# A chunked recurrence scan on one core: where one tile's products and one tile's turning stand among the steps of a matrix inverse

## The reference, cut to what matters

```python
def step(S, inp):
    d_t, k_t, v_t, kk_t, a_t = inp[:5]
    sa = jnp.einsum("bhvk,bhk->bhv", S, -kk_t)
    S = (S * d_t[:, :, None, :] + sa[..., None] * (kk_t * a_t)[:, :, None, :]
         + v_t[..., None] * k_t[:, :, None, :])
    out = jnp.einsum("bhvk,bhk->bhv", S, inp[5]) if emit else None
    return S, out
```

## Time and profile before

| what | value |
|---|---|
| runs of the kernel before | 2920.4 us median of 3 (2919.72 to 2921.86) |
| the profiled execution's own time | 2917.95 us |
| its span, first to last instruction | 2916.1 us |
| mean granted TensorE clock | 0.941 |
| PE busy / PEld busy | 89% / 68% of the span |
| DVE / ACT / POOL busy | 53% / 39% / 26% |
| the scan | about 1118 to 1818 us from the span's start |
| the profiled chain of work that ended last | names only the last instructions, so it says nothing of the scan |

### The profile page before, as it was taken

One profiled execution on the slowest core, in us unless ns is written; L12 is line 12 of the kernel. 1 busy time (PEld: TensorE's weight loads), 2 busy tenths in 40 slices (PEclk: granted clock), 3 DMA queues, 4 the chain that ended last, 5 costly groups with the idle time before them and its releaser, 6 DMA issues. The chain is left out here.

```text
span 2916.1 us, 66292 instructions
## 1 busy us (share of the span) xinstructions
PE 2599.0 (89%) x28644; PEld 1989.8 (68%) x28644; DVE 1542.1 (53%) x2689; ACT 1140.8 (39%) x1795; POOL 748.9 (26%) x436
## 2 busy tenths in 40 slices
PE   7998899979899996888888887989999999898987
PEld 5776588747678784777776775757788655476745
DVE  4634578883752313566565653334540366515995
ACT  4633332242452433455454443334422344423333
POOL 2413200002112125555444540122223200041201
PEclk9999899989789897899999998989999999999998
DMA  4224334233444441111111100542312100144431
GB/s 154 86 71 134 136 112 121 76 117 115 165 146 152 163 141 64 42 42 53 37 52 52 31 15 30 202 152 66 115 58 80 58 1 1 56 132 143 136 89 58
DMA packets 83661, 266.38 MB, mean 91 GB/s; under 512 B 11824, under 2 KB 12848, under 8 KB 82992
## 3 DMA queue, kind: packets, MB, share of 16 engines
q1 hardware_dynamic: 74160, 237.00, 25.3%
q10 hardware_dynamic: 9216, 25.17, 2.2%
HBM read 203.08 MB, written 36.70 MB: 82 GB/s over the span
## 5 line engine op out<-in xcount | busy, mean ns | idle before, releaser
L373 PE MATMUL ps<-h_parts_conv,w_parts_one 128*128 128x512 f32 x3168 | 582.1, 345 | 14.3 <-DVE h_parts_conv L359 12.4
L373 PEld LDWEIGHTS ps<-h_parts_conv,w_parts_one 128*128 128x128 f32 x3168 | 497.1, 192 | 103.5 <-DVE h_parts_conv L359 15.0
L373 PE MATMUL ps<-scratch_scan 64*64 64x64 f32 (+1 forms) x16704 | 387.3, 237 | 101.1 <-issue 47.4
L373 PEld LDWEIGHTS ps<-scratch_scan 64*64 64x64 f32 x16704 | 348.9, 139 | 147.6 <-issue 114.1
L441 POOL TENSOR_TENSOR w_parts_rwkv_out<-ring,w_parts_rwkv_out 128x1024 fp32r<-128x1024 f32 x78 | 186.3, 2390 | 789.0 <-ACT w_parts_rwkv_out L370 789.0
L441 POOL TENSOR_TENSOR w_parts_one<-ring,w_parts_one 128x1024 fp32r<-128x1024 f32 x82 | 202.9, 2475 | 684.1 <-ACT w_parts_one L370 683.9
L370 ACT ACTIVATE scratch_scan<-ps 128x384 f32<-128x384 f32 x560 | 243.0, 493 | 342.5 <-PE ps L373 189.9
L367 DVE SCALAR_TENSOR_TENSOR scratch_conv<-scratch_conv,vec 128x256 f32<-128x256 f32 (+1 forms) x656 | 332.4, 580 | 0.2
L373 PE MATMUL ps<-h_parts_attn,w_parts_rwkv_out 128*128 128x512 f32 (+1 forms) x1536 | 328.6, 373 | 0.0
L373 PEld LDWEIGHTS ps<-h_parts_attn,w_parts_rwkv_out 128*128 128x128 f32 x1536 | 264.0, 189 | 58.0 <-issue 10.1
L370 ACT ACTIVATE w_parts_rwkv_out<-ring 128x1024 fp32r<-128x1024 f32 x104 | 109.6, 1057 | 368.5 <-PE ps L373 338.1
(11 more groups left out here) (218 smaller groups left out, 3322.3 us busy)
## 6 DMA issues: line engine op xcount, KB each, us to landing
ring<-in_weights SPq DMA_DIRECT2D x311, 512.0 KB, 3.7
rwkv_spill<-scratch_conv ACTq DMA_DIRECT2D x64, 384.0 KB, 2.3
stream<-rwkv_spill SPq DMA_DIRECT2D x64, 384.0 KB, 3.6
scratch_conv<-scratch_conv SPq DMA_DIRECT2D x128, 103.1 KB, 2.2
scratch_conv<-scratch_conv SPq DMA_DIRECT2D x128, 67.4 KB, 2.0
x_spill<-stream SPq DMA_DIRECT2D x2, 3072.0 KB, 11.7
y_spill<-scratch_scan SPq DMA_DIRECT2D x8, 384.0 KB, 2.8
scratch_rwkv_out<-y_spill SPq DMA_DIRECT2D x8, 384.0 KB, 6.2
```

Of the source, the lines that this page charges most:

```text
L373: return nc.tensor.matmul(o, l, r, start=start, stop=stop)
```

## The change

On TensorE the products of `first_inverse` go from behind T(4) to behind Q(3), and the turning of a takes their place behind T(4), that is between level 4's two products. `FILLS` follows. On ScalarE the two copies of the turned a go from in front of `out_square` and the copies of P4 to behind the copies of T(4). On VectorE `p_start` is cut in two. The two masked copies keep the name and stand directly behind `inverse_update(w2, 3)`; the two additions of the identity become `p_diagonal` and stand behind `next_state(w3, 7)`. `normal_kk` goes from in front of `next_state(w3, 7)` to behind `next_state(w3, 8)`. No instruction is added or taken away.

```diff
-                 ("AT", 0), ("AT", 1), ("RC", 0), ("RC", 1), ("BO", 0), ("BO", 1), ("P4", 0), ("P4", 1), ("A", 0), ("A", 1),
+                 ("A", 0), ("A", 1), ("RC", 0), ("RC", 1), ("BO", 0), ("BO", 1), ("P4", 0), ("P4", 1), ("AT", 0), ("AT", 1),
...
                 Q(3)
-                both(a_turned, "AT")
+                at(first_inverse, "A", p)
                 chain(p, 7)
...
                 T(4)
-                at(first_inverse, "A", p)
+                both(a_turned, "AT")
                 chain(p, 9)
...
                     vtt(PQ[w % 2][:, h::2, :], bank3(fill_bank("A", w, h)), first_mask(w % 2)).then_inc(*read_inc("A", w, h))
+
+            def p_diagonal(w):
                 for h in range(2):
                     v.wait_ge(*read_at("A", w, h))
                     vtt(PQ[w % 2][:, h::2, :], PQ[w % 2][:, h::2, :], identb, ALU.add).then_inc(p_started, 1)
...
                 if two:
                     inverse_update(w2, 3)
-                if prep and wp % 2 == 0:
-                    normal_kk(wp // 2)
+                if one:
+                    p_start(w1)
                 if three:
                     next_state(w3, 7)
+                if one:
+                    p_diagonal(w1)
                 if one and w1 % 2 == 1:
                     for e in range(2):
                         bonus_values(w1 // 2, e)
                 if three:
                     next_state(w3, 8)
-                if one:
-                    p_start(w1)
+                if prep and wp % 2 == 0:
+                    normal_kk(wp // 2)
                 if three:
                     next_state(w3, 9)
...
                 T(3)
-                if two:
-                    a_turned(w2, 0)
-                    a_turned(w2, 1)
                 if read_pair is not None:
                     out_square(read_pair)
                 turned(4)
                 T(4)
+                if two:
+                    a_turned(w2, 0)
+                    a_turned(w2, 1)
```

## The result

The changed kernel takes 2900.69 us (median of 6 runs, 2894.97 to 2908.40), the kernel before beside it 2920.06 us (6 runs, 2916.93 to 2923.69). The ratio is 0.9934, 95% interval 0.9922 to 0.9945, so 19.3 us or 0.66% faster. Forecast were 2896.5 us and a gain of 23.8 us. A second measurement on another chip gave 0.9936 (0.9921 to 0.9952).

The account below looks back on a forecast made before the run. The scan was taken as bound by TensorE's program order and its waits, chiefly for VectorE's p_start queued ahead of Q(4)'s update. Terms of 13.8, 2.2, 1.8, 1.5 and 4.5 gave 23.8 us, so 2896.5 us; range 2886 to 2910.

Parts of the forecast that it names:

- rival 2: GpSimd becomes the bound of T(0), level 0 masked at 1429; gain 15 us in all, 2905 us; chance 0.17.
- odd periods 3 to 13: Wait for VectorE ahead of P5 goes, 2.3 us in each of six odd periods, 13.8 us.
- period 15: No normal_kk there and a wait of 0.93 us; 1.4 plus the clock, 2.2 us gained.
- period 1: First odd period of the scan's sum; 1.8 us gained.
- period 2: Has the long wait but no RC to cover the update ahead of P4; 1.5 us gained.
- even periods 4 to 14: Q(4), P5 and the outputs start earlier, 0.75 us in each of six periods, 4.5 us.
- TensorE's two moves: A and AT change places: chain 7 to T(4) starts 0.7 us earlier, T(4) to Q(4) gets 0.7 us longer.
- The additions, 0.95 us in odd periods: VectorE's two identity additions take 0.95 us where GpSimd waits for normal_kk, 2.15 in even periods.
- GpSimd, level 0 masked at 1427.8: GpSimd, released 3.2 us later in odd periods, masks level 0 between 1425.1 and 1427.8, upper end taken; T(0) wanted 1427.5.
- TensorE's clock, 0 to 1.3 us per odd period: With the wait ahead of P5 gone, the lower clock at P5's transposes may go, 0 to 1.3 us per period.
- 3 (the wait only moves): PE waits as long at T(0) or the next unit's first copies; gain below 6 us, 2915 to 2920; chance 0.06.
- 4: Slower: additions ahead of state 8 take 4.3 us beside GpSimd, delaying chain 9 and Q(4); 2935 us; chance 0.07.

Follow-up runs that it names:

- first pair: Profiled executions of the kernel before and the changed kernel, no further edit; the changed one took 2908.4 us, the slowest of its six.
- second pair: Kernel before and changed kernel, each with 128 empty TensorE instructions ahead of the scan, which do not show in the traces: 2926.35 and 2908.14 us.
- filler's run: Kernel before with 36 unused 64x64x64 matmuls added between Q(4) and chain 10 in odd periods: 2915.79 us, ratio 1.0011.

## Why the prediction was right, and where its sizes were off

The measured 2900.7 us lies in the range, and the forecast's case is the one that came, mixed with rival 2's mechanism at T(0). That the mechanism of the odd periods was right is shown; the total of 23.8 us owes its nearness also to the range, for the smaller terms failed. The terms of the sum can be measured from the end of Q(3) to the end of the next T(0), in the two pairs of traces:

| term, us | forecast | first pair | second pair |
|---|---|---|---|
| odd periods 3 to 13 | 13.8 | 14.1 | 12.6 |
| period 15 | 2.2 | 0.4 | 0.3 |
| period 1 | 1.8 | 0.2 | 0.2 |
| period 2 | 1.5 | -0.7 | 0.4 |
| even periods 4 to 14 | 4.5 | -2.7 | 2.8 |
| together | 23.8 | 11.3 | 16.3 |

Step by step, from end to end of the products in the trace:

- *TensorE's two moves, 0.7 us earlier and 0.7 longer.* Right. Where no pause fell in, Q(3) to T(4) went from 4.58 to 3.88 us, and T(4) to Q(4) in odd periods from 1.92 to 2.22.
- *P5 2.3 us earlier in odd periods.* Q(4) to P5 went from 3.12 to 1.13, as worked out. In all, Q(3) to P5 became 1.3 to 2.2 us shorter in periods 3 to 13, mean 1.8. What is missing to 2.3 are mostly pauses under issue, which fell inside A, AT or Q(4) in periods 3, 5, 7 and 9 (0.24 to 0.71 us each). The transposes at the upper clock level made up for it, so that the term 6 x 2.3 = 13.8 came out at 14.1 and 12.6.
- *The additions, 0.95 us in odd periods.* Right: 1.02. In even periods 2.59 instead of the 2.15 taken, still covered.
- *GpSimd, level 0 masked at 1427.8.* Right, upper end included. T(0) is released by GpSimd behind periods 1, 7, 11 and 13 (waits of 2.86, 0.80, 0.24 and 0.74 us); in period 7 at 1429.27, which is 1427.6 on the clock of the trace before. The rule of the Trainium skill (SBUF — State Buffer, section SBUF: two separate sides), that the two engines take turns, agrees with the 3.06 us for a scan of 1.747 and with 3.35 us for two additions of 0.55.
- *Period 1, 1.8 us.* Failed. P5 came 1.8 us earlier, but GpSimd, released later by `normal_kk`, then held T(0) for 2.86 us, where it had not held it before. I had worked out GpSimd's lateness for the later odd periods only.
- *Period 2, 1.5 us.* Failed. The long gap there, 2.02 us, was read as a wait for VectorE, but it stands inside Q(4), is put down to "issue" and lies on a mark of the ruler above. In the changed kernel it is still there (1.98 us). A wait for VectorE of like length lies hidden under it: in the filler's run, which has no pause at this place, chain 10 waits 1.85 us for the state update. Taking it away wins nothing while the pause stays.
- *Period 15, 2.2 us.* Failed. The wait of 0.93 us went, but a pause under issue came, 0.72 us inside Q(4) in the first pair and 1.47 us inside the outputs in the second, and in the first pair the transposes stayed at the lower level.
- *TensorE's clock, 0 to 1.3 us per odd period.* It came back: the stretch of the twelve transposes shows a granted clock of 1.00, and they take 1.53 us in period 7, as in all odd periods from 1 to 13. PE's busy time fell by 10.3 us in the first pair and 10.1 in the second, about half of the 19.3 us. What the clock is worth alone is left open: the filler run cannot tell, and the run with the turning back shows that the clock does not carry the gain without the waits.
- *Even periods, 0.75 us each.* Wrong in size. P5 came 1.3 us earlier only where no pause fell in, in period 14 (Q(3) to P5 8.76 before, 7.45 after); in periods 6 and 12 of the first pair it came 0.6 to 0.7 us later. The outputs waited for ScalarE's copy in four of the six, as forecast. The mean from Q(3) to T(0) over the seven even periods from 2 to 14 was 15.47 before and 15.96 after in the first pair, 15.60 and 15.15 in the second, where the term wanted 0.86 less. Period 6 of the first pair alone shows pauses of 0.48 and 0.76 us where there were none.
- *What I left out.* I took "issue" in the earlier trace rows as part of the stage and gave it no price. These pauses come at fixed distances in TensorE's stream of instructions, and they rose by 12.7 us in the first pair (46.9 to 59.6) and by 6.8 in the second (51.2 to 58.0), so they take back part of what is won elsewhere. This is the step that the forecast of periods 2, 15 and the even ones had wrong: it moved all work as if these places moved with it.

Of the rivals, 3 (the wait only moves) came true for a part: GpSimd's wait at T(0), once removed, moved into a pause. 4 did not occur in the changed kernel, but a single step of the queue was enough to bring it about.

## What to carry to other kernels

Where TensorE waits for another engine, read that engine's queue ahead of the instruction it waits for: here work for another unit stood there, and the gain came from moving it together with its producer. Such a move is one thing in parts: with the additions back in their old place 12.6 of the 19.3 us were left, with the turning back 5.3, with `normal_kk` back 2.9. The three losses add up to 37 us, more than the gain, so the parts lean on each other and none has a worth of its own. Moving a releaser later, as `normal_kk` here, also moves its consumer under other neighbours, so price the neighbours first.

## What the runs showed of the hardware that I had not expected

**TensorE's instructions arrive in packets, and the engine pauses at fixed distances in their stream.** The DMA view of the changed kernel, 1118 to 1818, columns packets, MB, share:

```profile
q8 instruction: 149, 2.44, 1.5%
```

They are 16 KB each. In the scan one starts every 4.1 us in the median, 4.5 in the mean. 149 packets for 18544 matmul records are one for every 124.5, which is the step of the ruler on which the pauses under "issue" stand. In time, too, they go together. Of the pauses over 0.25 us under "issue" between T(0) of period 1 and Q(4) of period 16, 51 of 52 before and 65 of 68 after end 2.0 to 3.0 us behind the start of a packet, 45.9 and 57.1 us in all. Of the pauses with a named releaser it is 14 of 71 and 12 of 57, near the 22% of all moments that lie so. Which matmul pauses is the same from run to run and from chip to chip (109 of 126), and it moves by half a step when half a packet of matmuls is put ahead. So the pauses belong to the packets' borders. That the engine waits there for the packet to arrive is what fits all this; I have not made packets come sooner and seen the pauses go, so that last step is supported, not shown.

**Chips differ more than this change is worth.** The changed kernel took 2900.7 us on one, 2895.4 us on another and, as its repeat, 2908.1 us on the third; the kernel before took 2920.1, 2912.9 and 2925.8 us there. Ratios to the kernel before on the same chip were 0.9934, 0.9936 and 0.9939.
